# Every second key page of the samples is turned in 32x32 blocks one stage earlier

## The reference

```
z = q.k / sqrt(64) + bias_h
A[t,s] = sigmoid(z[t,s]) * product over s < j < t of (1 - sigmoid(z[t,j]))      for s < t
o = A v
```

## Time and profile before

| what | value |
|---|---|
| median of 3 runs | 2328.16 us (2324.65 to 2330.84) |
| the profiled execution | 2329.63 us, of which the profile's span is 2327.9 us |
| PE, DVE, ACT busy over the span | 97%, 70%, 46% |
| granted clock of PE, mean | 0.993 |
| DMA over the span | 345.37 MB, mean 148 GB/s |
| DVE line 3333 (the block turns) | 64 instructions, 128x512 each |
| `k_blocks<-in_cache_k`, DRAM to DRAM | 64 DMAs of 256 KB |
| `w_page<-k_blocks` | 64 DMAs of 256 KB |

### The profile page before, as it was taken

The page is one execution under the profiler, slowest core; times in us unless marked ns, Lnnn a source line. Parts: engine busy times, 40 slices in busy tenths (PEclk is TensorE's granted clock), DMA queues, the critical chain, the costliest instruction groups (busy, mean ns, idle before and its releaser), DMA issues. The chain is left out here.

```text
span 2327.9 us, 43422 instructions
## 1 busy us (share of the span) xinstructions
PE 2248.4 (97%) x16494; PEld 1849.0 (79%) x16494; DVE 1623.8 (70%) x2755; ACT 1060.1 (46%) x1975; POOL 47.3 (2%) x107
## 2 busy tenths in 40 slices
PE   8999999999999999999989888999999999999998
PEld 8888888877879888888877665678977777777786
DVE  7676666757885487677667997556766766655886
ACT  7332232334564667566646564435422232324453
POOL 0000000000000100000010010010000000000000
PEclk9999999999999999999999999999999999999999
DMA  5343342465464445344448989532243432437354
GB/s 163 104 154 104 111 138 93 136 208 190 134 206 136 97 112 115 91 97 114 88 136 295 312 275 347 163 101 90 61 161 94 153 104 94 144 122 261 110 172 147
DMA packets 390830, 345.37 MB, mean 148 GB/s; under 512 B 105593, under 2 KB 298489, under 8 KB 390672
## 3 DMA queue, kind: packets, MB, share of 16 engines
q1 hardware_dynamic: 390672, 343.21, 47.7%
HBM read 271.54 MB, written 88.38 MB: 155 GB/s over the span
## 5 line engine op out<-in xcount | busy, mean ns | idle before, releaser
L1344 PE MATMUL a_q<-a_uh,a_p_hi 128*128 128x352 f32 x672 | 233.4, 347 | 0.6 <-ACT a_xp L1435 0.6
L1346 PE MATMUL a_q<-a_uh,a_p_lo 128*128 128x352 f32 x672 | 216.3, 322 | 0.0
L1345 PE MATMUL a_q<-a_ul,a_p_hi 128*128 128x352 f32 x672 | 215.9, 321 | 0.0
L1344 PEld LDWEIGHTS a_q<-a_uh,a_p_hi 128*128 128x128 f32 x672 | 126.5, 188 | 23.6 <-issue 21.7
L1345 PEld LDWEIGHTS a_q<-a_ul,a_p_hi 128*128 128x128 f32 x672 | 127.0, 189 | 0.1
L1346 PEld LDWEIGHTS a_q<-a_uh,a_p_lo 128*128 128x128 f32 x672 | 126.1, 188 | 0.0
L980 PE MATMUL c_q<-c_b_hi,c_a_hi 128*128 128x512 f32 x264 | 105.3, 399 | 3.6 <-DVE c_a_lo L879 2.3
L980 PE MATMUL a_q<-a_b_hi,a_a_hi 128*128 128x512 f32 x264 | 103.5, 392 | 2.0 <-DVE a_a_lo L879 1.8
L981 PE MATMUL c_q<-c_b_hi,c_a_lo 128*128 128x512 f32 x264 | 104.7, 397 | 0.0
L982 PE MATMUL c_q<-c_b_lo,c_a_hi 128*128 128x512 f32 x264 | 104.4, 395 | 0.0
L982 PE MATMUL a_q<-a_b_lo,a_a_hi 128*128 128x512 f32 x264 | 102.8, 389 | 0.0
(11 more groups left out here) (773 smaller groups left out, 6499.0 us busy)
## 6 DMA issues: line engine op xcount, KB each, us to landing
w_page<-in_cache_v SPq DMA_DIRECT2D x128, 256.0 KB, 4.4
a_w_raw<-in_ffn_gu SPq DMA_DIRECT2D x44, 512.0 KB, 5.1
c_w_raw<-in_ffn_gu SPq DMA_DIRECT2D x44, 512.0 KB, 5.0
a_a_raw<-hid_rows SPq DMA_DIRECT2D x66, 256.0 KB, 2.7
c_a_raw<-hid_rows SPq DMA_DIRECT2D x66, 256.0 KB, 2.7
k_blocks<-in_cache_k SPq DMA_DIRECT2D x64, 256.0 KB, 3.6
w_page<-in_cache_k SPq DMA_DIRECT2D x64, 256.0 KB, 4.0
w_page<-k_blocks SPq DMA_DIRECT2D x64, 256.0 KB, 5.0
```

The lines of the kernel that those rows point to most:

```text
L1344: nc.tensor.matmul(self.pm[at % 2][:, 0:TB], wh, self.uh[t][:, c], start=(c == 0), stop=False)
L1345: nc.tensor.matmul(self.pm[at % 2][:, 0:TB], wh, self.ul[t][:, c], start=False, stop=False)
L1346: mm = nc.tensor.matmul(self.pm[at % 2][:, 0:TB], wl, self.uh[t][:, c], start=False, stop=(c == KC - 1))
```

## The change

In the projection block SP now also loads each page of `k_blocks` after its rearranging copy has landed, VectorE turns it in 32x32 blocks, and SP stores it back to the same place of `k_blocks`. The buffers lie where the small inputs lay before and where `tail_nat` comes later, so the first load waits for `small_turned` and ACT's `rows_out` waits for the last stores. In the delta block the page is loaded as before, but the scores read it straight from its slot (`page`), VectorE's `key_copies` are gone, and a slot is refilled only once the scores of its round are done (`z_mm`); that place of the SP list moves from 0.74 to 2.7 behind the round's time. The eight first copies stand at 12, 18, ... 54; the load of page n at 86 + 5.2 n, its turn 3.4 later, its store at the place of the next load, and the copy of page n + 8 directly behind. Some semaphores are merged: `x` tiles 3 to 8 share one in pairs, and `gain_scaled` is counted in `gained`. The store of an attention result moves from 30.71 to 36.7.

```diff
+COPY_AT, BLOCK_AT = (12.0, 6.0), (86.0, 5.2)
+def block_time(n):
+    return BLOCK_AT[0] + BLOCK_AT[1] * n
...
@@ rows_out (ACT)
             yield unit_end(N_UNITS) + 3.7 + b
+            if b == 0:
+                for event, count in blocks_out:
+                    act.wait_ge(event, count)
...
@@ Attend.store (SP)
-            yield self.time(m, 30.71)
+            yield self.time(m, 36.7)
...
@@ first_half
+        KEY_BLOCKS = N_B // 2 * page_table.shape[1]
+        key_block, turned_block = yr.at("key_block", 17408, [P, SB]), [yr.at(f"turned_block{z}", 19456 + 2048 * z, [P, SB]) for z in range(2)]
...
-                sp.dma_start(xs[z][:], x[TILE0[i]:TILE0[i] + P, :]).then_inc(E(f"x_in{z}"), 16)
+                sp.dma_start(xs[z][:], x[TILE0[i]:TILE0[i] + P, :]).then_inc(E(f"x_in{z if z < 3 else 3 + (z - 3) // 2}"), 16)
...
@@ key_blocks (SP)
-                for n in range(N_B // 4 * page_table.shape[1]):
-                    gi, p = divmod(n, page_table.shape[1])
-                    yield 12.0 + 13.0 * n
+                numbers = []
+                for n in range(KEY_BLOCKS + 1):
+                    for m in range(8 if n == 0 else 0) if n == 0 else [n + 7]:
+                        if n == 0:
+                            yield COPY_AT[0] + COPY_AT[1] * m
+                            if m == 0:
+                                sp.wait_ge(E("blocks"), 16)
+                        elif m < KEY_BLOCKS:
+                            yield block_time(n - 1) + 0.1
+                        if m >= KEY_BLOCKS:
+                            continue
+                        if m % 2 == 0:
+                            numbers = page_numbers(nc, table, *divmod(m // 2, page_table.shape[1]), cache_k.shape[0])
+                        sp.dma_start(k_blocks[m].rearrange("(i t) (s d) -> (t s) i d", i=4, d=P),
+                                     cache_k[bass.ds(numbers[2 * (m % 2) + 1], 1)].rearrange("g k (i d) -> (g k) i d", d=P)).then_inc(E("blocks"), 16)
+                    yield block_time(n)
                     if n == 0:
-                        sp.wait_ge(E("blocks"), 16)
...
+                        sp.wait_ge(project.E("small_turned"), 1)
+                    else:
+                        sp.wait_ge(E("kb_turned"), n)
+                        sp.dma_start(k_blocks[n - 1], turned_block[(n - 1) % 2][:]).then_inc(E(f"kb_out{(n - 1) % 2}"), 16)
+                    if n < KEY_BLOCKS:
+                        sp.wait_ge(E("blocks"), 16 + 16 * min(n + 8, KEY_BLOCKS))
+                        sp.dma_start(key_block[:], k_blocks[n]).then_inc(E("kb_in"), 16)
...
@@ next_stage (SP), at 446
-                sp.wait_ge(E("blocks"), 16 + 32 * (N_B // 4 * page_table.shape[1]))
+                for z in range(2):
+                    sp.wait_ge(E(f"kb_out{z}"), 16 * KEY_BLOCKS // 2)
...
@@ input_norm (ACT)
-                    mean_square(0, z, xs[z][:], E(f"x_in{z}"), 16, sq1)
+                    mean_square(0, z, xs[z][:], E(f"x_in{z if z < 3 else 3 + (z - 3) // 2}"), 16 if z < 3 else 32, sq1)
...
@@ vector engine, first_half
+            def turn_keys():
+                for n in range(KEY_BLOCKS):
+                    yield block_time(n) + 3.4
+                    dve.wait_ge(E("kb_in"), 16 * (n + 1))
+                    at_least(dve, E(f"kb_out{n % 2}"), 16 * (n // 2))
+                    nc.vector.transpose(turned_block[n % 2][:], key_block[:]).then_inc(E("kb_turned"), 1)
...
@@ delta_and_sample: pages (SP)
-                        sp.wait_ge(E("k_turned0"), 2 * old + 2)
-                        sp.wait_ge(E("k_copied1"), 2 * old + 2)
+                        sp.wait_ge(E("z_mm"), scored(old))
...
@@ delta_and_sample: keys_of and scores (PE)
-                return k_turned[n % 2][:, b, :, rows_in(c)]
+                return page[n % SLOTS][:, b].rearrange("p (c n) -> p c n", n=P)[:, :, rows_in(c)]
...
-                        for e in range(2):
-                            pe.wait_ge(E(f"k_copied{e}"), 2 * (PAGES * gi + p) + 2)
+                        pe.wait_ge(E("k_copied0"), 2 * (PAGES * gi + p) + 2)
...
@@ delta_and_sample, vector engine
-            def key_copies():
-                for n, (gi, p) in enumerate(KEY_ROUNDS):
-                    for half in range(2):
-                        yield key_time(gi, p) + DVE_AT["key_copies"][half]
-                        if half == 0 and n >= 2:
-                            dve.wait_ge(E("z_mm"), turned_free(n))
-                        if half == 0:
-                            wait_page(dve, n)
-                        nc.vector.transpose(k_turned[n % 2][:, 2 * half + 1].rearrange("p c n -> p (c n)"),
-                                            page[n % SLOTS][:, 2 * half + 1]).then_inc(E("k_copied1"), 1)
```

More of the change, by code:

```diff
@@ L1469, in activate, with rows_out @@
             nc.scalar.preload_act_table_set("natural_log_exp_and_others")
-    def rows_out(self, act, sums_done):
+    def rows_out(self, act, sums_done, blocks_out):
         nc, E = self.nc, self.E
@@ L1981, in _ @@
                        project.evacuate(act, attend.E("z_mm"), attend.tiles_done), project.activate(act),
-                       project.rows_out(act, attend.E("o_mm")), attend.exponentials(act), attend.logs(act), attend.decays(act),
+                       project.rows_out(act, attend.E("o_mm"), [(E(f"kb_out{z}"), 16 * KEY_BLOCKS // 2) for z in range(2)]), attend.exponentials(act), attend.logs(act), attend.decays(act),
                        attend.copies(act, 0), attend.outs(act))
@@ L2007, in norms_out @@
                 dve.wait_ge(E("g_in"), 48)
-                nc.vector.tensor_scalar(g_post[:], g_post[:], 0.5, None, ALU.mult).then_inc(E("gain_scaled"), 1)
-                dve.wait_ge(E("gain_scaled"), 1)
+                nc.vector.tensor_scalar(g_post[:], g_post[:], 0.5, None, ALU.mult).then_inc(E("gained"), 1)
+                dve.wait_ge(E("gained"), 1)
                 for i in range(N):
@@ L2015, in norms_out @@
                     rstd = inverse(1, i)
-                    dve.wait_ge(E("gained"), i + 1)
+                    dve.wait_ge(E("gained"), i + 2)
                     dve.wait_ge(E(f"res_in{i % 2}"), 16 * (i // 2) + 16)
@@ L2032, in _ @@
             interleave(f.down_lo(dve), f.last_lo_parts(dve), f.last_unit_dve(dve), f.samples_dve(dve), f.step_sums(dve), f.down_adds(dve),
-                       norms_out(), norms_in(), turn2.dve(dve), project.rest_weights(dve), project.convolve(dve), project.turn_blocks(dve),
+                       norms_out(), norms_in(), turn2.dve(dve), project.rest_weights(dve), project.convolve(dve), project.turn_blocks(dve), turn_keys(),
                        attend.holds(dve), attend.weigh(dve), attend.scans(dve), attend.copies(dve, 1), attend.results(dve))
@@ L2497 @@
 ACT_AT = {"chain": (0.39, 3.41, 5.61, 7.0, 8.66, 10.05, -15.22), "advance": (4.41, 13.94), "gates": (-30.77, -41.18), "norms": (1.8, 3.3), "prepare": (-11.03, -9.42, -6.95, -35.25, -4.14, -2.8), "key_copies": (-0.12, 0.18), "weigh": (4.28, 11.47, 19.75), "weights": (0.21, -27.8), "head_norms": (24.61, 27.8)}
-DVE_AT = {"chain": (1.78, 4.08, 6.31, 7.59, -3.32, 9.05, -26.25, 10.9), "advance": (8.78, 15.6, 19.33), "gates": (-45.59, -26.31, -16.57), "norms": (2.18, 4.76), "prepare": (-10.62, -20.88, -5.18, -3.84, -1.84, -27.46), "key_copies": (0.33, -3.45), "logits": (2.42,), "weigh": (6.1, 13.38, 19.37, -26.87), "keep": (2.15,), "finish": (26.05, 30.08, 22.45, 25.02)}
+DVE_AT = {"chain": (1.78, 4.08, 6.31, 7.59, -3.32, 9.05, -26.25, 10.9), "advance": (8.78, 15.6, 19.33), "gates": (-45.59, -26.31, -16.57), "norms": (2.18, 4.76), "prepare": (-10.62, -20.88, -5.18, -3.84, -1.84, -27.46), "logits": (2.42,), "weigh": (6.1, 13.38, 19.37, -26.87), "keep": (2.15,), "finish": (26.05, 30.08, 22.45, 25.02)}
 POOL_AT = {"levels": (-57.98,)}
-SP_AT = {"pages": (0.74, 7.19), "chunk_rows": (-95.52, -10.93, 3.62, 10.18, 4.04), "attended": (8.41,), "head_gates": (13.73, 26.39), "first_rows": (5.4,)}
+SP_AT = {"pages": (2.7, 7.19), "chunk_rows": (-95.52, -10.93, 3.62, 10.18, 4.04), "attended": (8.41,), "head_gates": (13.73, 26.39), "first_rows": (5.4,)}
 def paced(at, n):
@@ L2612, in delta_and_sample, with scored @@
         row_norm = stage[0:T_S].rearrange("p z n -> p (z n)")
-        def turned_free(n):
-            gi, p = KEY_ROUNDS[n - 2]
+        def scored(n):
+            gi, p = KEY_ROUNDS[n]
             return ROUNDS * gi + p + 1
@@ L3090, in key_copies @@
                         if half == 0 and n >= 2:
-                            act.wait_ge(E("z_mm"), turned_free(n))
+                            act.wait_ge(E("z_mm"), scored(n - 2))
                         act.wait_ge(E("k_turned0"), 2 * n + half + 1)
@@ L3427, in _ @@
             nc.vector.memset(ones[:], 1.0)
-            interleave(queries(), masks_of_samples(), chain(), advance(), gates(), norms(), prepare(), key_copies(), logits(), weigh(), keep(), finish())
```

(1 more changed line is left out.)

5 lines of the change are left out of this document (removed).

## The result

| what | before | after |
|---|---|---|
| median | 2329.5 us (2324.65 to 2332.82) | 2397.89 us (2394.66 to 2404.24) |
| ratio, 95% interval | | 1.0292 [1.0267, 1.0316] |
| profiled execution, its span | 2329.63, 2327.9 us | 2395.29, 2393.6 us |
| mean granted clock | 0.993 | 0.983 |

A forecast was written before the change was run, and what follows sets the result against it. The prediction took TensorE to bound the projection block and VectorE the late key stage. Key stage -8, turns +7 and first tiles +1 sum to 0: 2329.6 us, given as 2329; range 2314 to 2352 us.

The forecast's parts named there:

- the wait of VectorE for the load in part 2: Projection block: the load lands within about 3.2 us, before VectorE's next turn needs it; no term charged.
- All have a unit's time in hand, so I cost them at nothing: Projection block: weight loads, row stores and result stores queued behind SyncE's new waits have slack; cost nothing.
- SyncE stops standing there: Projection block: an attention result's store, moved from 30.71 to 36.7, no longer makes SyncE wait; no gain by itself.
- Rival 1: Projection block: loads landing after 5.0 us pace VectorE, 6.1 us a cycle against 5.55; +24 us, 2354 us; chance 0.24.
- The turns' own work, 7 us: Projection block: 64 turns delay nine tight weighted tiles by 6 us in all, following copies add 1; 7 us.
- The traffic, 0: Projection block: 33.6 MB of loads and stores raise the DMA engines from 44% to 84% busy; no term.
- SP's wait for the turns, 0: Projection block: SyncE waits for each turn, planned 1.9 us before it asks; cost nothing.
- The key stage, -8 us: Delta block's key stage: removing the turns from VectorE shortens TensorE's waits; 8 us gained, bounded by 2.5 and 18.4.
- rival 3: Key stage: late page refills replace the turn as the last wait, gain of 8 shrinks to 2; 2336 us; chance 0.10.
- part of the two subtractions' wait is real latency: Key stage's delta chain: part of the subtractions' 5.9 us wait stays, roughly cancelled by shorter waits by way of ScalarE.
- The later slot, 0: Delta block: a slot is refilled 2.3 us later, yet its page lands 2.4 us before its turn; cost nothing.
- The first tiles, +1: Kernel start: the square of tile 3 waits for tile 4, to 18.2 us against 16.88; 1 us taken.

The follow-up runs named there:

- e5_uncoupled: Changed kernel with all 64 loads, stores and turns but no waits across engines, turning one page loaded once; 2342.09 us, 1.0047 of the kernel before.
- e7_sp_waits: e5_uncoupled with SP again waiting for each turn before the store and next load, VectorE waiting for no load; 2341.64 us, 1.0042.
- e3_turns_only: Changed kernel with the 64 projection-block turns all on one page loaded once, other loads and all stores out; 2341.68 us, 1.0031.
- e4_delta_only: Changed kernel without the projection block's page loads, turns, stores and their buffers, its copies kept; 2331.35 us, 1.0000.
- e2_dma_only: Changed kernel without the projection block's turns, pages loaded and stored back as they came from two buffers; 2329.23 us, 0.9997.
- e6_no_turn_early: Kernel before without its 64 delta-block turns, scores reading a constant, slots refilled at their old place; 2327.05 us, 0.9983.
- e9_four_buffers: Changed kernel with two landing and two turned buffers, pages from page 2 on loaded a cycle earlier, masks stored earlier; 2354.08 us, 1.0109.

## Why the prediction was wrong

**The step that failed** is the wait of VectorE for the load in part 2: "I take the value nearest to 2.7 and 3.6 us and charge no term of its own". It is 61 us of the 71.8 (536.5 in the change less 475.3 with the waits out), the lower clock included. Three things were wrong in it.

- The cycle was taken as even, 5.55 us each, with 3.2 us for the landing. Places in the lists are even in units, but between two turns VectorE has under 3 us of other work in 22 of 63 cases, and up to 9.3 us in others. In a closed round the longer of the gap and the round counts each time, and what a long gap gains is not carried over, since load n + 1 can't go before turn n. An estimate from the traces bears this out: 36 of the 63 spacings in e5_uncoupled are under 5.5 us, which is about the mean round of the change (turn 0.71, to the store 0.66, to the load 0.61, landing 3.56); with these raised to 5.5 the mean is 6.5 us, and 6.52 was measured. From 5.53 to 6.52 us over 63 is 62 us.
- The landing was taken as 2.7 to 3.6 us, though the same paragraph puts a price of 26 us on 3.6, and none was charged. The median of these loads is 3.4 us, so 0.2 above the bound of 3.2; where VectorE waited, issue to turn was 4.1 us. The 3.6 us of the earlier trace rows was no read into the core but a copy from DRAM to DRAM. The Trainium skill ("DMA: Bandwidth & Descriptors", "Anatomy of one DMA") states its fit of 2.0 us plus bytes over 436 GB/s for DMAs issued from GpSimd. SyncE issues these here, and the estimated 2.6 us that the prediction took from that fit is 0.8 us under the measured median. It would not have made the term 6 us instead of 7 either: by the prediction's own bound every landing within 3.2 us costs the same, nothing.
- "All have a unit's time in hand, so I cost them at nothing" held for what SP's waits do to others (e7_sp_waits: 0), but not for what stands between turn and load: 1.3 us in the mean, against the 0.43 of one issue that I counted. "SyncE stops standing there", said of the store of a result, did not come true either: it still stood 50.8 us for it between 770 and 1215 us, in 18 places.

**Rival 1 was the right mechanism with the wrong size.** "The round trip paces VectorE" had 24 us; it was 61. It asked for a landing of 4.4 us because it, too, compared means, and because its cycle holds one issue of 0.43 us where store and load are two. It had 36 us of standing where 72.7 were measured. That idle time hides a third of it was not too bold: 44% was hidden (41 us reached PE). What it had no term for is PE's clock, which added 19 us.

**The turns' own work, 7 us**: e3_turns_only costs 10.3 us over e4_delta_only, e5_uncoupled some 10. That it was lost at the nine tight tiles of the working was not looked at. **The traffic, 0**: none measured, with the DMA engines 67% busy in e2_dma_only where the prediction had 84%. **SP's wait for the turns, 0**: none in e7_sp_waits.

**The key stage, -8 us**: -4.1 in the change, -5.3 with its part alone, and neither is clear of the spread of 142.0 to 152.1 us. In the change PE did not even wait less. Here is the stage before, then after (columns as in the earlier trace rows):

```profile
1198.00:1345.00 147.00, 124.89 (x2594) 106.44 (x2595) 122.15 (x336) 84.55 (x204) 16.36 (x38) 0.94 0.81 275
```

```profile
1271.00:1415.00 144.00, 121.32 (x2604) 103.68 (x2605) 86.77 (x276) 85.26 (x206) 16.51 (x39) 0.98 0.84 277
```

VectorE has 35 us less to do, and PE's idle time is 22.1 us before and 22.7 after; what fell is its busy time, at a clock of 0.98 instead of 0.94. The waits in which VectorE's turns were named went, but the pages' loads came in their place, as rival 3 said, and ScalarE's part of the delta chain. Waits of PE in the key stage of the changed kernel:

```profile
PE b_D L2863 <- ACT b_p L3088: 3.6, 5, 1.8
PE b_S L2937 <- ACT w_turned_rows L3125: 3.5, 1, 3.5
PE b_S L2937 <- DMA w_page<-k_blocks: 2.8, 4, 1.0
```

The second of them was there before as well. In e4_delta_only and e6_no_turn_early PE's idle time did fall, to 18.5 and 17.6 us. Taking all turns out and keeping the early slots (e6_no_turn_early) gives a stage no shorter, though no wait of PE in it names a page's load; its longest are 3.5 us for ScalarE's page copy and 3.0 and 2.3 us in the delta chain. That points to the chain and not to the pages as what holds the rest. That "part of the two subtractions' wait is real latency" fits this, since e6_no_turn_early still has 2.9 of their 5.9 us; that waits by way of ScalarE would get shorter does not.

**The later slot, 0**: no cost shown. **The first tiles, +1**: the square of tile 3 starts at 18.87 us instead of 16.88, where the working gave 18.2. Whether the +1.6 us ahead of the units come from it is not shown: in e6_no_turn_early, whose start is that of the kernel before, the units begin at 710.5 us, later than the 709.9 of the change, and in the other runs between 709.8 and 712.8.

**What stays open.** What causes the 12 waits that are left with four buffers was not separated: the landings, VectorE work that SP stands for, or SP's wait for the newest copy, which no run took out. That the even gap alone would mend the change was not tried: it needs other places in VectorE's list for its other work. No version here that does all the work beats the kernel before; the best form of the whole change is e9_four_buffers, at 1.0109.

## What to carry to other kernels

When work goes into the list of an in-order engine with a wait for a transfer, draw the round first: what must happen between this use and the next load's issue, which queues stand in it, and how many buffers of lead it has. Then compare the round with the shortest run-time gap between two uses in that engine's list, not with the mean one; at every gap below the round the engine stands, and all that is queued behind the wait stands with it. Two buffers at each end belong to such a move from the start, and the stage that is to gain deserves a run without the work, since here it had 0.2% to give. Before a few us of one stage in one trace are called a gain, compare its idle time and its clock apart, and look how far the stage moves between runs that do the same in it.

## What the hardware showed

PE's granted clock fell after its idle time, not in it. Around the wait shown above (columns as in the earlier trace rows):

```profile
842.00:846.00 4.00, 0.56 (x4) 0.26 (x2) 0.18 (x1) 0.57 (x2) 0.00 (x0) 1.00 0.89 294
846.00:850.00 4.00, 3.10 (x12) 3.10 (x13) 4.00 (x8) 2.19 (x2) 0.00 (x0) 0.57 0.55 176
850.00:854.00 4.00, 4.00 (x40) 3.61 (x40) 4.00 (x9) 1.48 (x5) 0.00 (x0) 1.00 0.07 21
```

PE is all but idle for 4 us at a clock of 1.00; in the next 4 us the mean is 0.57, most of it at the lower of its two levels, 1.2 GHz, and matmuls of 0.32 us take up to 0.64; then it is back at 2.4 GHz. Over the units this turned 47.6 us of added idle time into 71.0 us of added length, so a wait that PE sees costs here, in the mean, half as much again as it lasts. And 33.6 MB of traffic more, at 178 GB/s and 67% busy DMA engines, took nothing that can be told from zero (e2_dma_only).
